# Linear-attention heads with tokens on the partitions behind the decay, in a two-block transformer kernel

## The chip, the cores and the metric

The kernel runs on one core of one Trainium2 chip. The metric is the device time of one execution in microseconds (us), as the median over runs. Engines are named as in the profile: PE (TensorE matmul), PEld (its weight loads), DVE (VectorE), ACT (ScalarE), SP (SyncE, which starts weight transfers).

## What is computed

The reference is a stack of two model blocks on one sequence of 256 tokens with 2048 features, all in float32. The first block's mixer projects the normed input by `w_in` into seven parts: `ka`, `qa`, `va`, `oa` for four linear-attention (mLSTM) heads of width 256 that run forward and backward in time, and `qb`, `kb`, `vb` for eight neighbourhood-attention heads. The change touches only the four mLSTM heads. In the closed form that the kernel uses, one head with the forward and the backward direction d is:

```
P_d[s, t] = (k_s . q_t) * scale * exp(col_d[s] + row_d[t])   for s <= t (d = forward), s >= t (d = backward), else 0
num_d[t, :] = sum_s P_d[s, t] * v[s, :]
den_d[t]    = sum_s P_d[s, t]
h[t, :] = sum_d num_d[t, :] / max(|den_d[t]|, exp(-m_d[t]))
out[t, :] = h[t, :] * rsqrt(mean(h[t, :]^2) + eps) * g_head * sigmoid(oa[t, :])
```

256 tokens are two chunks of 128. Of the four 128x128 blocks of P_d one is zero for each direction: keys in the later chunk against queries in the earlier for the forward direction, and the reverse for the backward.

## The kernel before

It is written engine by engine, with semaphores. Weights come as 412 **pieces** of 1 MB (128x2048). SP loads a piece into one of four `raw` slots when TensorE has finished the piece four before it. ACT's `split` rounds it to `w_hi` (L999), and DVE's `split` subtracts to get `w_lo` (L1412, on top of `raw`). TensorE multiplies each piece with the high and low halves of the activations. All three engines walk the same list of pieces. ACT and DVE call `begin(stage, j)` at each piece j; it does the split of the piece two ahead (`AHEAD = 2`) before anything else. ACT's split waits until TensorE has finished the piece before the present one (three `w_hi` slots). `begin` on DVE then also does the **ada** work placed at that piece by the table `ADA_AT`: the modulation vectors of later layers are matrix-vector products done on DVE, two instructions (L1425) for each 512 KB ada piece, one or two ada pieces at each weight piece, and at every eighth ada piece a transpose and a reduction more (L1431, L1432).

In a stage of columns (`ka`, `qa`, `qb`, `kb`, `oa`) each piece gives one bank of results. ACT copies half of it (`first_half`, L1018), and DVE adds the other half (`second_half`, L1465), which frees the bank. In a stage of tokens (`va`, `vb`) ACT evicts after four pieces, and DVE has no eviction.

Between the pieces stand the steps of the mLSTM heads. The table `A_STEPS` says behind which piece each step stands, on every engine: `scores`, `mix` and `norm` of head 0 at (va, 7), (qb, 1), (qb, 3), of head 1 at (qb, 4), (qb, 6), (kb, 0), of head 2 at (kb, 1), (kb, 3), (kb, 5), of head 3 at (kb, 6), (vb, 0), (vb, 2). The TensorE part of a step stands after the matmuls of that piece, the DVE part after its `second_half`, the ACT part after its `first_half`.

- `scores`: TensorE makes the products of k and q for both directions (L659), and spreads two rows of the gates over all partitions (L663: 512 columns, the row of the decay and the row of the bound). DVE adds the mask, ACT takes exponentials (L1072; L1074 for the bound), DVE multiplies by the scores (L1586). Keys are on the partitions.
- `mix`: TensorE multiplies `va` (stationary) with P (moving, 256 tokens) for the numerators (L680), and a block of ones with P for the denominators, which so stand on all 128 partitions (L676). Features are on the partitions. DVE then works on 128x512 tiles: bound, reciprocal, two products, sum, square (L1592 to L1598).
- `norm`: TensorE sums the squares over the partitions with a block of ones (L688). DVE makes the mean (L1602), ACT the root (L1078), DVE the reciprocal (L1604) and the product into `an` (L1606).

The neighbourhood-attention heads follow as waves from (vb, 3) on; the first (`b_wave(0)`, L721) waits until all four mLSTM heads are in `an`, because it reuses the PSUM banks `px`.

## Time and profile before

| | before |
|---|---|
| median of 3 runs | 2487.39 us (2486.23 to 2492.87) |
| the profiled execution | 2484.72 us |
| its span, first to last instruction | 2482.9 us |
| PE busy | 2375.4 us, 96% |
| DVE busy | 1996.0 us, 80% |
| ACT busy | 1109.2 us, 45% |
| granted TensorE clock, mean | 0.986 of full speed |

Times in rows are in us from the start of the span, unless marked ns. A timeline row has the start, the duration, the engine, the line, the operation, output<-inputs, shapes, and in brackets the idle time before it with what ended it; rows in sequence that are alike are merged (x4), and then the duration is that of all. A float32 matmul shows as two matmul records. A row of the stages has the stretch, its length, the busy time of each engine with the number of records, the granted clock (1.00 is 2.4 GHz, 0.50 is 1.2 GHz), the share of the DMA engines and GB/s. A row of groups has busy us and mean ns of one, and idle time before it. Ends of matmuls are modelled, so the distance between the starts of two rows tells how long the first took.

### The profile page before, as it was taken

The numbers are of one execution on the slowest core, as the hardware profiler recorded it, in microseconds if no ns is written. First come the engines' busy times: TensorE is split into PE (matmuls) and PEld (weight loads), VectorE is DVE, ScalarE is ACT, GpSimd is POOL, SyncE is SP. The second block draws the span as 40 slices with busy tenths as digits, with TensorE's granted clock in tenths as the row PEclk, the third lists the DMA queues.
The fourth block names the chain that finished last, engine by engine and source line by source line (L and its number), as shares of the span: only waits on it lengthen the run. The fifth ranks groups of instructions, "written<-read, shape, count | busy, mean of one in ns | idle before, by whom it ended". The sixth has DMA issues, their size and how long they took to land.

```text
span 2482.9 us, 31940 instructions
## 1 busy us (share of the span) xinstructions
PE 2375.4 (96%) x12936; PEld 2047.2 (82%) x12936; DVE 1996.0 (80%) x2481; ACT 1109.2 (45%) x1364; POOL 0.2 (0%) x4
## 2 busy tenths in 40 slices
PE   3599999998999999999998999999999998999999
PEld 3588887887888888888887788888888887888987
DVE  8999998899888888877787888787787666884764
ACT  1233434544445434454444444643545333555552
POOL 0000000000000000000000000000000000000000
PEclk9699999999999999999999999999999999999999
DMA  9889766685777688667685888776777775664343
GB/s 393 336 317 342 256 220 201 233 302 207 263 261 263 216 291 307 238 243 244 224 271 193 300 317 313 264 242 216 262 254 255 270 265 182 233 211 163 117 170 136
DMA packets 119010, 620.16 MB, mean 250 GB/s; under 512 B 13392, under 2 KB 14672, under 8 KB 76112
## 3 DMA queue, kind: packets, MB, share of 16 engines
q1 hardware_dynamic: 70560, 446.30, 51.3%
q10 hardware_dynamic: 48304, 171.82, 19.1%
q8 instruction: 102, 1.67, 0.3%
q14 instruction: 44, 0.36, 0.0%
HBM read 615.98 MB, written 2.10 MB: 249 GB/s over the span
## 4 chain that ended last, share of the span: by engine, by line
PE 72%; DVE 21%; DMA 3%; ACT 3%; issue 1%; ACTq 0%; SPq 0%; DVEq 0%
PE pm L536 20%; PE pm L537 10%; PE ps L536 10%; DVE w_lo L1412 7%; PE ps L537 5%; DVE acc L1425 5%; PE pm L575 4%; PE pm L576 4%; PE pm L577 4%; DMA ada<-in_ada 2%; ACT w_hi L999 2%; PE ps L575 2%; PE ps L577 2%; PE ps L576 2%; DVE acc_first L1478 1%
## 5 line engine op out<-in xcount | busy, mean ns | idle before, releaser
L1412 DVE TENSOR_TENSOR w_lo<-raw,w_hi 128x2048 fp32r<-128x2048 f32 (+2 forms) x412 | 892.0, 2165 | 296.1 <-ACT w_hi L999 294.4
L999 ACT ACTIVATE w_hi<-raw 128x2048 fp32r<-128x2048 f32 (+2 forms) x412 | 746.8, 1813 | 452.1 <-DMA raw<-in_w_down 128.3
L536 PE MATMUL pm<-h,w_hi 128*128 128x512 f32 x2350 | 832.6, 397 | 6.5 <-DVE w_lo L1412 6.3
L537 PE MATMUL pm<-h,w_lo 128*128 128x256 f32 x2350 | 658.0, 280 | 0.0
L536 PEld LDWEIGHTS pm<-h,w_hi 128*128 128x128 f32 x2350 | 440.9, 188 | 116.9 <-issue 13.0
L1425 DVE SCALAR_TENSOR_TENSOR acc<-ada,csil,acc 128x512 f32<-128x512 f32 x600 | 449.7, 749 | 12.6
L537 PEld LDWEIGHTS pm<-h,w_lo 128*128 128x128 f32 x2350 | 443.6, 189 | 0.2
L536 PE MATMUL ps<-h,w_hi 128*128 128x512 f32 x1202 | 426.4, 397 | 1.1 <-DVE w_lo L1412 1.0
L537 PE MATMUL ps<-h,w_lo 128*128 128x256 f32 x1202 | 336.5, 280 | 0.0
L536 PEld LDWEIGHTS ps<-h,w_hi 128*128 128x128 f32 x1202 | 225.5, 188 | 56.7 <-issue 3.6
L537 PEld LDWEIGHTS ps<-h,w_lo 128*128 128x128 f32 x1202 | 226.9, 189 | 0.1
L536 PE MATMUL pm<-glu,w_hi 128*128 128x512 f32 x484 | 170.5, 395 | 0.0
L575 PE MATMUL pm<-w_hi,h 128*128 128x512 f32 x352 | 138.9, 395 | 8.9 <-DVE h L1515 5.1
L576 PE MATMUL pm<-w_lo,h 128*128 128x512 f32 x352 | 137.8, 391 | 0.0
L577 PE MATMUL pm<-w_hi,h 128*128 128x512 f32 x352 | 137.6, 391 | 0.0
L537 PE MATMUL pm<-glu,w_lo 128*128 128x256 f32 x484 | 136.0, 281 | 0.0
L536 PEld LDWEIGHTS pm<-glu,w_hi 128*128 128x128 f32 x484 | 90.8, 188 | 21.7 <-DVE w_lo L1412 0.2
L537 PEld LDWEIGHTS pm<-glu,w_lo 128*128 128x128 f32 x484 | 91.1, 188 | 0.0
L591 PE MATMUL pv<-ones,acc_first 128*128 128x1 f32 x128 | 26.6, 338 | 66.5 <-DVE mods L1449 49.8
L1198 ACT ACTIVATE conv<-conv 128x256 f32<-128x256 f32 x44 | 18.4, 418 | 157.1 <-DVE conv L1715 157.1
L575 PEld LDWEIGHTS pm<-w_hi,h 128*128 128x128 f32 x352 | 66.6, 189 | 24.2 <-issue 5.5
L591 PEld LDWEIGHTS pv<-ones,acc_first 128*128 128x128 f32 x128 | 26.4, 313 | 66.8 <-DVE acc_first L1478 50.1
(403 smaller groups left out, 3100.8 us busy)
## 6 DMA issues: line engine op xcount, KB each, us to landing
ada<-in_ada ACTq DMA_DIRECT2D x320, 512.0 KB, 5.4
raw<-in_w_up SPq DMA_DIRECT2D x88, 1024.0 KB, 5.0
raw<-in_w_in SPq DMA_DIRECT2D x56, 1024.0 KB, 5.5
raw<-in_w_down SPq DMA_DIRECT2D x64, 704.0 KB, 5.0
raw<-in_sgu_v SPq DMA_DIRECT2D x32, 1024.0 KB, 6.0
raw<-in_sgu_u SPq DMA_DIRECT2D x32, 1024.0 KB, 5.2
raw<-in_sgu_z SPq DMA_DIRECT2D x32, 1024.0 KB, 4.9
raw<-in_sgu_out SPq DMA_DIRECT2D x32, 1024.0 KB, 4.9
```

Source lines behind the costliest of these rows:

```text
L536: pe.matmul(dst[:, :], wh[:, k, :], hl, start=(kc == 0), stop=False, skip_group_check=True)
L537: mm = pe.matmul(dst[:, 0:T], wl[:, k, :], hi, start=False, stop=last, skip_group_check=True)
L575: pe.matmul(dst[:, :], h_hi, wh[:, k, :], start=(kc == 0), stop=False, skip_group_check=True)
L576: pe.matmul(dst[:, :], h_hi, wl[:, k, :], start=False, stop=False, skip_group_check=True)
L577: mm = pe.matmul(dst[:, :], h_lo, wh[:, k, :], start=False, stop=(kc == 4 * parts - 1), skip_group_check=True)
L591: mm = pe.matmul(pv[:, c:c + 1], acc_first[:, u % 2, r, c * P:(c + 1) * P], ones[:, 0:1], start=(r == 0), stop=(r == 1))
L999: act.activation(w_hi[:, q % HSLOTS, 0:n], raw[:, q % SLOTS, 0:n], ACT.Copy).then_inc(hi_ready, 1)
L1198: act.activation(conv[:, k % 2, :], conv[:, k % 2, :], ACT.Gelu).then_inc(gelu_ready, 1)
L1412: tt_(w_lo[:, q % SLOTS, 0:n], raw[:, q % SLOTS, 0:n], whole(w_hi[:, q % HSLOTS, 0:n]), ALU.subtract).then_inc(lo_ready, 1)
L1425: ins = stt(dst, w, c, dst, ALU.mult, ALU.add)
L1478: ins = stt(dst, w, c, dst, ALU.mult, ALU.add)
```

## The change

Behind the decay the heads now have tokens on the partitions.

- `scores`: the bound no longer comes as a spread row. L663 has 256 columns instead of 512. The bound is turned once, by two more small transposes behind (ka, 7), and its exponential is taken once by ACT, at (qa, 0). L1074 is gone.
- `mix`: P is now the stationary operand, in 128x128 blocks, and `va` the moving one (256 columns). Each block is also multiplied with one column of ones, which gives the denominator as one column. The zero blocks are left out: 6 blocks a head instead of 8. DVE works on 128x4 for the denominators and with per-partition scalars on four 128x256 tiles.
- Squares and their sums are made by ACT (`accum_out`), in a new step `A_SQUARES` one piece after `mix`; ahead of ACT's `first_half` of that piece. Behind it DVE makes the mean (after its `second_half`), and ACT the root (after its `first_half`).
- `norm`: DVE makes a diagonal of the reciprocal roots (128x128 twice), ahead of its `second_half` of the norm's piece but behind its `begin`. TensorE multiplies h with the diagonal, which scales and turns it back to features on the partitions (four matmuls of 128 columns). DVE multiplies by `g_head`.

```diff
@@ -134,6 +134,7 @@
            ("kb", 6): ("scores", 3), ("vb", 0): ("mix", 3), ("vb", 2): ("norm", 3)}
+A_SQUARES = {("qb", 2): 0, ("qb", 7): 1, ("kb", 4): 2, ("vb", 1): 3}
 B_WAVES = {("vb", 3): 0, ("vb", 4): 1, ("vb", 5): 2, ("vb", 7): 3, ("oa", 0): 4, ("oa", 1): 5, ("oa", 2): 6, ("oa", 3): 7,
...
@@ -225,9 +226,10 @@
         bias_b = work("bias_b", [P, NH_B * 6, GRID_W], 14848)
-        expm = at_("expm", [P, 2, T], o_nt)
-        hf = at_("hf", [P, 2, T], o_nt + 2 * T)
-        bcol = at_("bcol", [P, TT, GROW], o_ssq)
+        diag_a = at_("diag_a", [P, TT, P], o_nt)
+        hf = at_("hf", [P, TT, DH_A], o_nt + 2 * T)
+        bcol = at_("bcol", [P, 2, TT, GROW], o_ssq + 160)
+        small_a = at_("small_a", [P, 4, 4], o_ssq + 304)
         wmask = at_("wmask", [P, GRID_W], o_ssq + 80)
...
@@ -653,14 +658,14 @@
                 else:
-                    pe.wait_ge(a_sq, hd_)
+                    pe.wait_ge(a_hf, hd_)
                 for sc in range(TT):
                     for dc in range(2):
                         pe.matmul(px[0][:, sc * T:(sc + 1) * T], ka[:, 2 * hd_ + dc, sc * P:(sc + 1) * P],
                                   qa[:, 2 * hd_ + dc, :], start=(dc == 0), stop=(dc == 1))
                 for d in range(2):
                     r = hd_ + 32 * d
-                    mm = pe.matmul(px[1 + d][:, :], ident[0:GROW, r:r + 1].to_broadcast([GROW, P]), neg_rows[0:GROW, :],
+                    mm = pe.matmul(px[1 + d][:, 0:T], ident[0:GROW, r:r + 1].to_broadcast([GROW, P]), neg_rows[0:GROW, 0:T],
                                    start=True, stop=True)
...
@@ -670,23 +675,25 @@
                 else:
-                    pe.wait_ge(a_ms, hd_)
-                for d in range(2):
-                    for sc in range(TT):
-                        pe.matmul(px[3][:, d * T:(d + 1) * T], ones[:, :], decay[:, d, sc * T:(sc + 1) * T],
-                                  start=(sc == 0), stop=(sc == 1))
-                    for ec in range(2):
-                        for sc in range(TT):
-                            mm = pe.matmul(px[1 + d][:, ec * T:(ec + 1) * T],
-                                           va[:, sc, hd_ * DH_A + ec * P:hd_ * DH_A + (ec + 1) * P],
-                                           decay[:, d, sc * T:(sc + 1) * T], start=(sc == 0), stop=(sc == 1))
+                    pe.wait_ge(a_out, hd_)
+                for tc in range(TT):
+                    for d in range(2):
+                        seen = range(tc + 1) if d == 0 else range(tc, TT)
+                        for sc in seen:
+                            first, last = sc == seen[0], sc == seen[-1]
+                            probs = decay[:, d, sc * T + tc * P:sc * T + (tc + 1) * P]
+                            pe.matmul(px[3][:, 2 * tc + d:2 * tc + d + 1], probs, ones[:, 0:1], start=first, stop=last)
+                            mm = pe.matmul(px[1 + d][:, tc * DH_A:(tc + 1) * DH_A], probs, va[:, sc, hd_ * DH_A:(hd_ + 1) * DH_A],
+                                           start=first, stop=last)
                 mm.then_inc(a_num, 1)
 
             def a_head_norm(hd_):
-                pe.wait_ge(a_sq, hd_ + 1)
+                pe.wait_ge(a_diag, hd_ + 1)
                 for ec in range(2):
-                    mm = pe.matmul(px[3][:, 0:T], ones[:, :], hb[:, ec, :], start=(ec == 0), stop=(ec == 1))
-                mm.then_inc(a_ss, 1)
+                    for tc in range(TT):
+                        mm = pe.matmul(px[3][:, ec * T + tc * P:ec * T + (tc + 1) * P], hf[:, tc, ec * P:(ec + 1) * P], diag_a[:, tc, :],
+                                       start=True, stop=True)
+                mm.then_inc(a_turned, 1)
 
...
@@ -729,7 +736,9 @@
                     for sc in range(TT):
-                        mm = pe.transpose(px[1][:, sc * GROW:(sc + 1) * GROW], gates[0:GROW, 5, sc * P:(sc + 1) * P],
+                        pe.transpose(px[1][:, sc * GROW:(sc + 1) * GROW], gates[0:GROW, 5, sc * P:(sc + 1) * P],
+                                     ident[0:GROW, 0:GROW])
+                        mm = pe.transpose(px[1][:, (TT + sc) * GROW:(TT + sc + 1) * GROW], neg_rows[0:GROW, T + sc * P:T + (sc + 1) * P],
                                           ident[0:GROW, 0:GROW])
...
@@ -1069,13 +1078,19 @@
                     for sc in range(TT):
-                        act.activation(decay[:, d, sc * T:(sc + 1) * T], decay[:, d, sc * T:(sc + 1) * T], ACT.Exp,
-                                       bias=bcol[:, sc, r:r + 1])
-                    act.activation(expm[:, d, :], px[1 + d][:, T:2 * T], ACT.Exp).then_inc(a_exp, 1)
-
-            def a_head_norm(hd_):
+                        ex = act.activation(decay[:, d, sc * T:(sc + 1) * T], decay[:, d, sc * T:(sc + 1) * T], ACT.Exp,
+                                            bias=bcol[:, 0, sc, r:r + 1])
+                    ex.then_inc(a_exp, 1)
+
+            def a_head_squares(hd_):
+                act.wait_ge(a_hf, hd_ + 1)
+                for tc in range(TT):
+                    sq = act.activation(hb[:, tc, :], hf[:, tc, :], ACT.Square, accum_out=small_a[:, 1, tc:tc + 1])
+                sq.then_inc(a_sq, 1)
+
+            def a_head_root(hd_):
                 act.wait_ge(a_ms, hd_ + 1)
-                act.activation(expm[:, 0, :], expm[:, 0, :], ACT.Sqrt).then_inc(a_std, 1)
+                act.activation(small_a[:, 2, 0:TT], small_a[:, 2, 0:TT], ACT.Sqrt).then_inc(a_std, 1)
 
...
@@ -1113,9 +1128,10 @@
                     b_exponent(B_WAVES[part, j] - 1)
+                if (part, j) in A_SQUARES:
+                    a_head_squares(A_SQUARES[part, j])
                 if (part, j) == ("vb", 0):
                     act.wait_ge(rows_ready, 1)
-                    act.wait_ge(bcol_ready, 1)
                 if (part, j) == ("oa", 6):
...
@@ -1136,9 +1152,13 @@
                     mix_high(hx[:, 2:4, 0:T], ob, 2)
-                if (part, j) in A_STEPS and A_STEPS[part, j][0] != "mix":
-                    step, k = A_STEPS[part, j]
-                    {"scores": a_head_scores, "norm": a_head_norm}[step](k)
+                if (part, j) == ("qa", 0):
+                    act.wait_ge(bcol_ready, 1)
+                    act.activation(flat(bcol[:, 1, :, :]), flat(bcol[:, 1, :, :]), ACT.Exp).then_inc(ecol_ready, 1)
+                if (part, j) in A_STEPS and A_STEPS[part, j][0] == "scores":
+                    a_head_scores(A_STEPS[part, j][1])
+                if (part, j) in A_SQUARES:
+                    a_head_root(A_SQUARES[part, j])
                 if (part, j) in B_WAVES:
...
@@ -1571,7 +1591,7 @@
                     dve.wait_ge(bcol_ps, 1)
-                    dve.tensor_copy(flat(bcol[:, :, :]), px[1][:, 0:2 * GROW]).then_inc(bcol_ready, 1)
+                    dve.tensor_copy(bcol[:, :, :, :].rearrange("p a b c -> p (a b c)"), px[1][:, 0:4 * GROW]).then_inc(bcol_ready, 1)
 
...
@@ -1587,23 +1607,36 @@
                 dve.wait_ge(a_num, hd_ + 1)
-
-                em = flat(expm[:, :, :])
-                chain.link(stt(em, px[3][:, :], -1.0, em, ALU.mult, ALU.max))
-                chain.link(tt_(em, px[3][:, :], em, ALU.max))
-                chain.link(dve.reciprocal(em, em))
-                tt_(hf[:, :, :], halves(px[1][:, :]), over(expm[:, 0, :], 2), ALU.mult)
-                chain.link(tt_(hb[:, :, :], halves(px[2][:, :]), over(expm[:, 1, :], 2), ALU.mult))
-                chain.link(tt_(hf[:, :, :], hf[:, :, :], hb[:, :, :], ALU.add))
-                tt_(hb[:, :, :], hf[:, :, :], hf[:, :, :], ALU.mult).then_inc(a_sq, 1)
+                if hd_ == 0:
+                    dve.wait_ge(ecol_ready, 1)
+                den, bound = halves(px[3][:, 0:4]), bcol[:, 1, :, hd_:hd_ + 33:32]
+                norm = halves(small_a[:, 0, :])
+                chain.link(stt(norm, den, -1.0, bound, ALU.mult, ALU.max))
+                chain.link(tt_(norm, den, norm, ALU.max))
+                chain.link(dve.reciprocal(small_a[:, 0, :], small_a[:, 0, :]))
+                for tc in range(TT):
+                    ins = ts_(hf[:, tc, :], px[1][:, tc * DH_A:(tc + 1) * DH_A], small_a[:, 0, 2 * tc:2 * tc + 1], None, ALU.mult)
+                chain.link(ins)
+                for tc in range(TT):
+                    ins = stt(hf[:, tc, :], px[2][:, tc * DH_A:(tc + 1) * DH_A], small_a[:, 0, 2 * tc + 1:2 * tc + 2], hf[:, tc, :],
+                              ALU.mult, ALU.add)
+                ins.then_inc(a_hf, 1)
+
+            def a_head_mean(hd_):
+                dve.wait_ge(a_sq, hd_ + 1)
+                ts_(small_a[:, 2, 0:TT], small_a[:, 1, 0:TT], 1.0 / DH_A, EPS, ALU.mult, ALU.add).then_inc(a_ms, 1)
+
+            def a_head_diagonal(hd_):
+                dve.wait_ge(a_std, hd_ + 1)
+                chain.link(dve.reciprocal(small_a[:, 3, 0:TT], small_a[:, 2, 0:TT]))
+                for tc in range(TT):
+                    ins = ts_(diag_a[:, tc, :], ident[:, :], small_a[:, 3, tc:tc + 1], None, ALU.mult)
+                ins.then_inc(a_diag, 1)
 
             def a_head_norm(hd_):
-                dve.wait_ge(a_ss, hd_ + 1)
-                ts_(expm[:, 0, :], px[3][:, 0:T], 1.0 / DH_A, EPS, ALU.mult, ALU.add).then_inc(a_ms, 1)
-                dve.wait_ge(a_std, hd_ + 1)
-                chain.link(dve.reciprocal(expm[:, 0, :], expm[:, 0, :]))
+                dve.wait_ge(a_turned, hd_ + 1)
                 for ec in range(2):
-                    ins = stt(an[:, 2 * hd_ + ec, :], hf[:, ec, :], pcol("ghead", 2 * hd_ + ec), expm[:, 0, :], ALU.mult, ALU.mult)
+                    ins = ts_(an[:, 2 * hd_ + ec, :], px[3][:, ec * T:(ec + 1) * T], pcol("ghead", 2 * hd_ + ec), None, ALU.mult)
                 ins.then_inc(a_out, 1)
...
@@ -1653,6 +1686,8 @@
                     chain.link(tt_(bias_b[:, :, :], bias_b[:, :, :], over(wmask[:, :], NH_B * 6), ALU.add))
+                if (part, j) in A_STEPS and A_STEPS[part, j][0] == "norm":
+                    a_head_diagonal(A_STEPS[part, j][1])
                 if (part, j) == ("oa", 7):
...
@@ -1665,6 +1700,8 @@
                     {"scores": a_head_scores, "mix": a_head_mix, "norm": a_head_norm}[step](k)
+                if (part, j) in A_SQUARES:
+                    a_head_mean(A_SQUARES[part, j])
                 if (part, j) in B_WAVES and B_WAVES[part, j] < NH_B:
```

Two places show where the steps now stand. The first is ACT's queue at head 0, from the split at (qb, 2) to the split at (qb, 3); `w_hi<-raw` is a split, `qb<-pm` a `first_half`, `ada<-in_ada` the start of an ada transfer. Before:

```order
L999 ACTIVATE w_hi<-raw 128x2048 [waits slot_full0,piece_done]
L1004 DMA ada<-in_ada 128x1024 [waits ada_used]
L1018 ACTIVATE qb<-pm 128x256 [waits piece_done]
L999 ACTIVATE w_hi<-raw 128x2048 [waits slot_full1,piece_done]
L1004 DMA ada<-in_ada 128x1024 [waits ada_used]
L1018 ACTIVATE qb<-ps 128x256 [waits piece_done]
L1078 ACT_TABLE_LOAD
L1078 ACTIVATE expm<-expm 128x256 [waits a_ms]
```

and with the change:

```order
L1008 ACTIVATE w_hi<-raw 128x2048 [waits slot_full0,piece_done]
L1013 DMA ada<-in_ada 128x1024 [waits ada_used]
L1088 ACTIVATE sqt,small_a<-hf 128x256 [waits a_hf]
L1088 ACTIVATE sqt,small_a<-hf 128x256
L1027 ACTIVATE qb<-pm 128x256 [waits piece_done]
L1093 ACT_TABLE_LOAD
L1093 ACTIVATE small_a<-small_a 128x2 [waits a_ms]
L1008 ACTIVATE w_hi<-raw 128x2048 [waits slot_full1,piece_done]
```

The root, which waits for DVE's mean (`a_ms`), now stands ahead of the second split, where it stood behind it; the two squares (they write `sqt` as a by-product) stand ahead of the `first_half`.

The second is DVE's queue, from the split at (qb, 3) to the next split; `w_lo<-raw` is a split, `acc<-ada` the ada work, `qb<-qb` a `second_half`, `qa` is where `an` lies. Before:

```order
L1412 TENSOR_TENSOR w_lo<-raw,w_hi 128x2048 [waits hi_ready]
L1425 SCALAR_TENSOR_TENSOR acc<-ada,csil,acc 128x512 [waits ada_full2]
L1425 SCALAR_TENSOR_TENSOR acc<-ada,csil,acc 128x512 [waits dve_step]
L1465 TENSOR_TENSOR qb<-qb,ps 128x256 [waits half_out,ada_used]
L1602 TENSOR_SCALAR expm<-px 128x256 [waits a_ss]
L1604 RECIPROCAL expm<-expm 128x256 [waits a_std]
L1606 SCALAR_TENSOR_TENSOR qa<-hf,par,expm 128x256 [waits dve_step]
L1606 SCALAR_TENSOR_TENSOR qa<-hf,par,expm 128x256
L1412 TENSOR_TENSOR w_lo<-raw,w_hi 128x2048 [waits hi_ready]
```

and with the change, from the mean at (qb, 2) on:

```order
L1627 TENSOR_SCALAR small_a<-small_a 128x2 [waits a_sq]
L1432 TENSOR_TENSOR w_lo<-raw,w_hi 128x2048 [waits hi_ready]
L1445 SCALAR_TENSOR_TENSOR acc<-ada,csil,acc 128x512 [waits ada_full2]
L1445 SCALAR_TENSOR_TENSOR acc<-ada,csil,acc 128x512 [waits dve_step]
L1631 RECIPROCAL small_a<-small_a 128x2 [waits a_std,ada_used]
L1633 TENSOR_SCALAR diag_a<-ident,small_a 128x128 [waits dve_step]
L1633 TENSOR_SCALAR diag_a<-ident,small_a 128x128
L1485 TENSOR_TENSOR qb<-qb,ps 128x256 [waits half_out]
L1639 TENSOR_SCALAR qa<-px,par 128x256 [waits a_turned]
L1639 TENSOR_SCALAR qa<-px,par 128x256
```

The diagonal stands behind a split and the ada work, and the two products into `qa` behind a wait for TensorE's turn. TensorE's own place of the norm's matmuls, behind the piece (qb, 3), is as before; they waited for the squares made in `mix` and now wait for the diagonal.

## Rows read from the trace of the kernel before

**Rows 1.** Busy time in the mLSTM stretch: PE, PEld, DVE, ACT, POOL, clock, DMA

```profile
250.00:410.00 160.00, 156.00 (x788) 129.32 (x787) 146.62 (x157) 66.63 (x77) 0.00 (x0) 0.99 0.67 235
```

**Rows 2.** Timeline of PE: start of the piece (qb, 3), and what follows it

```profile
277.09 0.39 PE L536 MATMUL ps<-h,w_hi 128*128 128x512 f32 x1
...
282.64 1.03 PE L688 MATMUL px<-sqt,ones 128*128 128x256 f32 x4
```

**Rows 3.** What PE waited for, 380 to 410: total us, times, longest

```profile
PE px L721 <- ACT vb L1132: 2.4, 1, 2.4
PE pm L575 <- DVE w_lo L1412: 1.1, 1, 1.1
PE px L688 <- DVE sqt L1598: 0.5, 1, 0.5
```

**Rows 4.** Timeline of PE: end of scores of head 0, mix of head 1

```profile
253.04 1.98 PE L663 MATMUL px<-neg_rows,ident 36*128 36x512 f32 x4
254.95 0.50 PE L536 MATMUL ps<-h,w_hi 128*128 128x512 f32 x1
...
304.30 1.02 PE L676 MATMUL px<-decay,ones 128*128 128x256 f32 x4
...
309.29 0.58 PE L536 MATMUL pm<-h,w_hi 128*128 128x512 f32 x1
```

**Rows 5.** Timeline of PE near 57: float32 matmuls of one column, full clock

```profile
56.66 1.84 PE L591 MATMUL pv<-ones,acc_first 128*128 128x1 f32 x16
```

**Rows 6.** Timeline of DVE at head 1, (qb, 6) to (kb, 0)

```profile
309.67 0.69 DVE L1592 SCALAR_TENSOR_TENSOR expm<-px,expm 128x512 f32<-128x512 f32 x1
...
317.17 2.29 DVE L1412 TENSOR_TENSOR w_lo<-raw,w_hi 128x2048 fp32r<-128x2048 f32 x1
319.37 1.54 DVE L1425 SCALAR_TENSOR_TENSOR acc<-ada,csil,acc 128x512 f32<-128x512 f32 x2
...
322.41 0.42 DVE L1465 TENSOR_TENSOR qb<-qb,pm 128x256 f32<-128x256 f32 x1
322.75 2.28 DVE L1412 TENSOR_TENSOR w_lo<-raw,w_hi 128x2048 fp32r<-128x2048 f32 x1
324.95 0.48 DVE L1423 TENSOR_SCALAR acc<-ada,csil 128x512 f32<-128x512 f32 x1
...
327.83 0.42 DVE L1465 TENSOR_TENSOR kb<-kb,pm 128x256 f32<-128x256 f32 x1
```

**Rows 7.** Timeline of ACT at head 0, (qb, 2) to (qb, 4)

```profile
277.29 0.38 ACT L1018 ACTIVATE qb<-pm 128x256 f32<-128x256 f32 x1 [7.15 <-PE pm L537]
...
288.23 1.90 ACT L999 ACTIVATE w_hi<-raw 128x2048 fp32r<-128x2048 f32 x1
```

**Rows 8.** Groups of DVE by form: eviction with a scalar, diagonal

```profile
L1602 DVE TENSOR_SCALAR expm<-px 128x256 f32<-128x256 f32 x4 | 1.7, 419 | 0.0
...
L1832 DVE TENSOR_SCALAR diag<-ident,stat 128x128 f32<-128x128 f32 x4 | 1.1, 286 | 0.1
```

**Rows 9.** Timeline of ACT, then of DVE, at wave 0: table load, tiny reciprocal

```profile
411.80 1.28 ACT L1101 ACT_TABLE_LOAD   x1 [2.18 <-DVE acc L1425]
413.15 0.51 ACT L1101 ACTIVATE s_b<-s_b,small_b 128x256 f32<-128x256 f32 x1
...
415.22 0.16 DVE L1615 RECIPROCAL small_b<-small_b 128x2 f32<-128x2 f32 x1
```

**Rows 10.** Short stretches around three waits of PE; the granted clock is third from the end

```profile
406.00:407.00 1.00, 0.00 (x0) 0.00 (x0) 0.96 (x2) 1.00 (x2) 0.00 (x0) 0.99 0.49 164
...
412.00:414.00 2.00, 2.00 (x7) 1.57 (x6) 1.93 (x4) 1.93 (x4) 0.00 (x0) 0.55 0.76 207
...
1352.00:1354.00 2.00, 0.00 (x0) 0.00 (x0) 1.96 (x2) 0.00 (x0) 0.00 (x0) 0.62 0.00 0
...
1358.00:1360.00 2.00, 2.00 (x8) 1.58 (x7) 2.00 (x6) 1.80 (x2) 0.00 (x0) 0.68 0.00 0
...
1379.00:1381.00 2.00, 0.34 (x2) 0.00 (x0) 2.00 (x1) 1.72 (x1) 0.00 (x0) 1.00 0.98 385
```

5 lines of the change are left out of this document (4 added, 1 removed).

## The prediction

> **What bounds the kernel now.** I read the page's first part (the table above): TensorE is the busiest engine by far. Then the stage, since the average says nothing of it: from 250 to 410 us, where nearly all the mLSTM work lies, TensorE is busy for 156 of 160 us, DVE for 146.6, ACT for 66.6 [rows 1]. So TensorE is the bound there and DVE is close behind it; DVE's work counts only where TensorE waits for it. The waits of TensorE in this stage add up to 4.0 us and all lie near the end [rows 3]: 0.5 us for the squares of head 3, 1.1 us for a `w_lo` that DVE made late, 2.4 us before wave 0. The last is put down to ACT's eviction, but that wave also waits for head 3 in `an`, DVE's last product of the norm, which the code names (`a_out`). All three come from DVE being late.
>
> That last wait costs more than its length. The granted clock is still 0.99 in 406 to 407, and 0.55 in 412 to 414, which is full speed again from about 413.7 on [rows 10]. So it was granted 1.2 instead of 2.4 GHz from 407.0 to 413.7. TensorE had stopped near 405.5 and worked again from 407.9: 5.8 us of work at half speed, 2.9 us lost. Another wait, at 1352 to 1358, shows the same length: 0.62 in one stretch and 0.68 in the other put the low clock from 1352.5 to 1359.3, some 6.8 us [rows 10]. A third, shorter one, with TensorE idle for 1.7 of the 2 us from 1379, keeps 1.00 [rows 10].
>
> **The change, part by part. TensorE's own work.**
> - Scores: L663 takes 1.90 us a head, from 253.04 to the next row [rows 4]; half the columns, half the time: -0.95 a head, -3.8.
> - Mix: from 304.30 to 309.29 it takes 4.99 us for 24 records of 256 columns, 0.208 each [rows 4]. Now 6 blocks have 12 such records, 2.5 us, and 12 records of one column. A train of 16 of those took 1.84 us, 0.115 each [rows 5]: 1.4 us. Sum 3.9, so -1.1 a head, -4.4. Were the short ones hidden behind the long ones, it would be 2.5 (-2.5 a head), and that is the lower bound; the upper is 0.208 for all 24 records, no gain. I take 0.115, the row of the same shape.
> - The Trainium skill, page "TensorE: Matmul & The Clock Gate", section "Back-to-back issue gap", gives small matmuls an issue floor of some 25 ns. By it the mix would be about 2.8 us (an estimate from the page); the row, at 115 ns, speaks against it, since each record here also loads 128 columns of float32 weights.
> - Norm: 4 records of 256 columns become 8 of 128, 0.9 us either way. The two extra transposes at (ka, 7) cost about 0.2 us. Together: -3.8 - 4.4 + 0.2 = -8.0 us.
>
> **DVE's work.** The mix on DVE lasts from 309.67 to 317.17, 7.5 us [rows 6]. Now: three operations on 128x4 at about 0.2 (the tiny reciprocal takes 0.16 [rows 9]), and four passes of 128x256 at 0.42 [rows 8] with the ends overlapping: 2.25 us. The norm loses a 1.75 us reciprocal too. DVE gets some 7 us a head lighter, and is then never late at the three waits above: -4.0 and -2.9 of clock, -6.9 us.
>
> **The new wait.** This is the part that decides. Until now TensorE needed for the norm only the squares that DVE made within `mix`, two pieces earlier. Now it needs the diagonal, and between the mix and the diagonal stand two of DVE's `begin`s, two trips to ACT and one of ACT's splits: the order shows DVE's mean, then ACT's root, and behind the root ACT's split, for which DVE's next split waits, then the ada work, then the diagonal. For head 1, from the end of TensorE's mix:
> - DVE: mix 2.25; split 2.2; ada work of (qb, 7) with transpose and reduction 3.0 (319.37 to 322.41); `second_half` 0.35; mean 0.2 [rows 6, 9]: 8.0.
> - ACT: root of 128x2 about 0.2, its table load being done meanwhile; split 1.9 [rows 7]: 10.1.
> - DVE: split 2.2; ada work of (kb, 0) 2.9 (324.95 to 327.83) [rows 6]; tiny reciprocal 0.2 [rows 9]; two diagonals 0.29 each, overlapping, 0.5 [rows 8]: 15.9.
> - TensorE meanwhile: two pieces of 5.55 (277.09 to 282.64) [rows 2] and some 0.1, 11.2.
>
> So TensorE waits for 4.7 us at head 1. Head 2 has two whole ada pieces (3.1) in the first `begin` and 3.0 in the second: 5.0. Head 0 has one ada piece each time (1.5), but DVE comes 1.2 us late to its mix from work before: 3.2. At head 3 the pieces are of the `vb` kind, and DVE and ACT don't wait for a `first_half` there: 2.25 + 2.2 + 1.5 + 0.2 + 0.2, ACT's split 1.9, DVE's 2.2, ada 1.5, diagonal 0.7 is 12.7, against two pieces of 5.44: 1.8. Sum +14.7 us. Nothing hides these: the norm's matmuls stand in TensorE's queue ahead of the next piece. ACT's squares (0.5 each [rows 9]) end before its `first_half` is due, and the extra exponential at (qa, 0), 0.3 us, falls in a stage where ACT is idle for more than half: no cost; were that cover gone, it would be 0.3 us and a table load, 1.6.
>
> A page differs here: the Trainium skill, "ScalarE: Activation LUTs", section "What ACT_TABLE_LOAD costs", gives 2.66 us for a change of table, load and drain. By that the root would be late by itself and the waits about 3 us longer in all (an estimate from the page). The row shows 1.28 us, and the next activation starts 0.07 us after its end [rows 9], so I go by that.
>
> **The clock.** If each wait longer than 2.4 us is followed by the low clock, and it lasts 6.7 us from some 1.6 us into the wait (1.5 after 405.5), then a wait of s leaves 6.7 - (s - 1.6) of work at half speed: half of that is 2.55 for head 0, 1.8 for head 1, 1.65 for head 2, nothing for head 3 (1.8 us is like the wait that kept 1.00). Sum +6.0. Bounds: 0 if it never falls, and 4 x 2.9 = 11.6 if each costs what the one before wave 0 cost.
>
> **Sum.** -8.0 - 6.9 + 14.7 + 6.0 = +5.8 us. Behind the stage the engines stand as before, TensorE going from piece to piece, so it is carried to the end. Against the profiled execution, 2484.72 us, that is 2490.5; the median of the runs shown lies 2.7 us above that execution, so 2493.2 us for the median. A measurement of this kernel can tell about 0.3%, 7.5 us, from no change. I forecast no measurable change, a little on the slow side.
>
> **Rivals.**
> - A, slower: the clock. The wait is as forecast, but at each of the four norms the clock falls and stays low through the norm and half of the next piece. For it: the one comparable wait in a stage dense with pieces, of 2.4 us, cost 2.9. Against: longer waits use up part of the low time. It gives +5.8 - 6.0 + 11.6 = +11.4 us, 2498.8. It decides from a low time of about 4 us of work after each wait.
> - B, faster: the wait is not there. If the diagonal came by the time that TensorE ends the norm's piece, only the savings are left: -8.0 - 6.9 = -14.9 us, 2472.5. For it: DVE sheds 7 us a head and could be well ahead. Against: being ahead doesn't help, as the root can't come before the piece before is evicted and DVE's split waits for ACT's. From the end of that piece it is at least 0.2 (ACT starts at 277.29 what TensorE ended at 277.09 [rows 2, 7]), 0.4 + 0.4 + 0.2 + 0.2 (both halves, mean, root), 1.9, 2.2, 1.5 and 0.7, together 7.7, against 5.55 of the norm's piece.
> - C, the one-column records are hidden behind the long ones, the lower bound above: the mix takes 2.5 us, -1.4 a head more, of which head 0 gives its part back in waiting: +5.8 - 4.2 = +1.6 us, 2489.0. Against it: the train of sixteen [rows 5]. The rule of the Trainium skill's page on TensorE would come near this.
>
> **How the numbers follow.** The forecast, 2487 to 2496: 0.52. A: 0.30. B: 0.10. C: 0.08. Of the forecast's 0.52 some 0.08 lies over the 7.5 us bound. So faster 0.10 (B), within 0.3% 0.44 + 0.08 = 0.52, slower 0.30 + 0.08 = 0.38. For the range I take in the forecast, C and A: the lower end is the waits with no clock lost, 5.8 - 6.0 = -0.2, and half of C's gain, 2485, rounded down to 2484 for a first wait that is shorter; the upper is A and 2 us more for DVE's small operations, 2501. B is left out.
>
> **What would show it.** Right: a wait of TensorE at the norm's matmuls (L694 in the changed code) for DVE's diagonal, four times, 2 to 5 us; the three waits of [rows 3] gone; the granted clock at 0.5 after the longer ones; DVE's busy time in the stage down by some 27 us; the mix at 3.9 us. Wrong: no such wait, or one under 1 us, would make it B. A wait that moves to `w_lo` behind the norm would say that ACT's split, held up by the root, is late for TensorE too.

## Result and the profile after

| | before | changed |
|---|---|---|
| median | 2487.68 us (2486.23 to 2492.87, 6 runs) | 2496.45 us (2492.77 to 2499.75, 6 runs) |
| ratio to before, 95% interval | | 1.0031 [1.0021, 1.0041] |
| the profiled execution | 2484.72 us | 2492.77 us |
| its span | 2482.9 us | 2490.9 us |
| DVE busy | 1996.0 us | 1969.7 us |
| granted clock, mean | 0.986 | 0.984 |

The changed kernel is slower by 8.8 us, 0.31 to 0.35%: in the range, 3.3 us above the forecast, just past the 0.3% that I called no measurable change, and 0.45 us over the upper end of the forecast's own 2487 to 2496. By its number it stands a little nearer to rival A (2498.8) than to the forecast (2493.2). What PE waited for in the changed kernel from 240 to 430 us is one line (total us, times, longest), in the place of the three of [rows 3]:

```profile
PE px L694 <- DVE diag_a L1633: 15.6, 4, 5.0
```

The stretches of the changed kernel, with the columns of [rows 1] and [rows 10]; the first answers to [rows 1]:

```profile
250.00:410.00 160.00, 144.44 (x763) 123.19 (x762) 117.98 (x161) 65.04 (x82) 0.00 (x0) 0.96 0.64 220
284.00:286.00 2.00, 1.40 (x10) 1.30 (x10) 1.04 (x5) 0.00 (x0) 0.00 (x0) 0.91 0.98 311
286.00:288.00 2.00, 2.00 (x8) 1.71 (x7) 2.00 (x3) 0.00 (x0) 0.00 (x0) 0.50 0.40 160
288.00:290.00 2.00, 2.00 (x11) 1.78 (x10) 1.97 (x3) 0.00 (x0) 0.00 (x0) 0.74 0.00 0
327.00:329.00 2.00, 1.92 (x9) 1.92 (x10) 0.36 (x2) 0.00 (x0) 0.00 (x0) 0.50 0.85 207
329.00:331.00 2.00, 2.00 (x10) 1.72 (x10) 1.80 (x3) 0.00 (x0) 0.00 (x0) 0.75 0.50 195
...
369.00:371.00 2.00, 1.49 (x7) 1.49 (x8) 0.79 (x3) 0.00 (x0) 0.00 (x0) 0.50 0.54 123
371.00:373.00 2.00, 2.00 (x8) 1.80 (x8) 1.37 (x3) 0.00 (x0) 0.00 (x0) 0.50 0.35 139
373.00:375.00 2.00, 2.00 (x9) 1.66 (x8) 2.00 (x2) 0.00 (x0) 0.00 (x0) 0.66 0.00 0
```

DVE is busy for 28.6 us less in 250 to 410. Not all of that is relief, since less of the stage's work now falls into that stretch: over the whole kernel DVE is busy for 26.3 us less (1996.0 to 1969.7), 6.6 us a head, where about 7 were foreseen. TensorE stands still for 15.6 of the 160 us, where it stood for 4. The third number from the end is the clock. Behind the waits at heads 0, 1 and 2 (work resumes at 284.60, 327.08 and 369.51) it is at 0.50, which is 1.2 GHz, up to about 289.0, 330.0 and 374.4. The work done in that time lost half of it: 1.7, 1.45 and 2.4 us, in all 5.6. Behind head 3's wait of 2.0 us it did not fall.

The timeline of PE in the changed kernel, at the mix of head 0 and then at the norm of head 1:

```profile
265.51 0.28 PE L685 MATMUL px<-ones,decay 128*128 128x1 f32 x2
265.65 0.68 PE L686 MATMUL px<-va,decay 128*128 128x256 f32 x2
266.17 0.28 PE L685 MATMUL px<-ones,decay 128*128 128x1 f32 x2
...
269.25 0.58 PE L541 MATMUL pm<-h,w_hi 128*128 128x512 f32 x1
```

```profile
327.08 2.08 PE L694 MATMUL px<-diag_a,hf 128*128 128x128 f32 x8 [4.88 <-DVE diag_a L1633]
328.81 0.77 PE L541 MATMUL ps<-h,w_hi 128*128 128x512 f32 x1
```

The mix now takes 3.74 us (4.99 in [rows 4]): from start to start, 0.14 us for the pair of one-column records of a block and 0.52 for the pair of 256 columns. The turn at the norm took 1.73 us here, at the low clock; at head 0, with the clock at 1.00, it took 0.92, and the norm's matmuls before took 0.68 (282.64 to 283.32).

Now the chain that makes TensorE wait, at head 1. DVE in the changed kernel:

```profile
311.14 0.16 DVE L1614 SCALAR_TENSOR_TENSOR small_a<-px,bcol 128x4 f32<-128x4 f32 x1 [2.85 <-PE px L686]
...
313.45 2.28 DVE L1432 TENSOR_TENSOR w_lo<-raw,w_hi 128x2048 fp32r<-128x2048 f32 x1
...
319.02 0.16 DVE L1627 TENSOR_SCALAR small_a<-small_a 128x2 f32<-128x2 f32 x1
321.26 2.29 DVE L1432 TENSOR_TENSOR w_lo<-raw,w_hi 128x2048 fp32r<-128x2048 f32 x1 [2.08 <-ACT w_hi L1008]
323.47 0.48 DVE L1443 TENSOR_SCALAR acc<-ada,csil 128x512 f32<-128x512 f32 x1
323.99 2.33 DVE L1445 SCALAR_TENSOR_TENSOR acc<-ada,csil,acc 128x512 f32<-128x512 f32 x3
326.35 0.17 DVE L1631 RECIPROCAL small_a<-small_a 128x2 f32<-128x2 f32 x1
326.55 0.48 DVE L1633 TENSOR_SCALAR diag_a<-ident,small_a 128x128 f32<-128x128 f32 x2
```

and ACT beside it:

```profile
316.69 0.39 ACT L1027 ACTIVATE qb<-pm 128x256 f32<-128x256 f32 x1 [2.21 <-PE pm L542]
317.10 1.28 ACT L1093 ACT_TABLE_LOAD   x1
319.22 0.20 ACT L1093 ACTIVATE small_a<-small_a 128x2 f32<-128x2 f32 x1 [0.84 <-DVE small_a L1627]
...
319.33 1.90 ACT L1008 ACTIVATE w_hi<-raw 128x2048 fp32r<-128x2048 f32 x1
```

The root is done at 319.4. The diagonal, which needs only the root, starts at 326.35: DVE idles for 2.08 us for ACT's split, does its own split (2.2 us) and four ada instructions (2.9), because the diagonal stands behind them in its queue. TensorE had ended its piece at 322.2. DVE was idle 2.85 us before the mix, so it is not overloaded at this head.

**Where the time went.** I take the stage from the first product of q and k to the start of wave 0, in the timeline of PE: 251.2 to 407.9 before, 251.2 to 416.8 now, 156.7 against 165.6 us, +8.9. Its terms, measured: scores 4 x (1.05 - 1.91) = -3.4; mix 4 x (3.74 - 4.99) = -5.0; the old waits gone, -4.0; the new ones +15.6; low clock +5.6. Sum +8.8. Not in it is the turn, 0.1 to 0.2 us a head longer than the norm's matmuls before, which is within what the pieces themselves differ by. Behind the stage the low clock after the wait before wave 0 (2.9 us) is gone. The spans differ by +8.0, so 2.0 us are left over, which lie at places that the change does not touch.

### The profile page after: what moved, and what is told of

It reads as the page before. It is cut to its first block, busy times and chain, and to the rows that moved or that the text cites. A ratio compares the mean times of both kernels' runs of the same rounds, so it can differ in the third digit from the quotient of the medians.

```text
span 2490.9 us, 31993 instructions
## 1 busy us (share of the span) xinstructions
PE 2372.5 (95%) x12954; PEld 2047.8 (82%) x12954; DVE 1969.7 (79%) x2489; ACT 1112.8 (45%) x1373; POOL 0.2 (0%) x4
## 4 chain that ended last, share of the span: by engine, by line
PE 75%; DVE 18%; DMA 3%; ACT 2%; issue 1%; ACTq 0%; SPq 0%; DVEq 0%
PE pm L541 21%; PE pm L542 11%; PE ps L541 11%; DVE w_lo L1432 7%; PE ps L542 5%; PE pm L580 4%; PE pm L581 4%; PE pm L582 4%; DVE acc L1445 4%; ACT w_hi L1008 2%; DMA ada<-in_ada 2%; PE ps L580 2%; PE ps L581 2%; PE ps L582 2%; DVE nt L1527 1%
## 5 line engine op out<-in xcount | busy, mean ns | idle before, releaser
L1445 DVE SCALAR_TENSOR_TENSOR acc<-ada,csil,acc 128x512 f32<-128x512 f32 x600 | 449.4, 749 | 12.6
L1218 ACT ACTIVATE conv<-conv 128x256 f32<-128x256 f32 x44 | 18.5, 420 | 157.2 <-DVE conv L1752 157.2
```

The source lines that it names most:

```text
L1218: act.activation(conv[:, k % 2, :], conv[:, k % 2, :], ACT.Gelu).then_inc(gelu_ready, 1)
L1445: ins = stt(dst, w, c, dst, ALU.mult, ALU.add)
```

## Experiments

Times taken at different hours are compared by their ratios to the kernel before, which ran beside each. The stage is measured as above, in one profiled execution of each version; two versions without a wait in it (e1 and e10) agree within 0.02 us. A "load" is unused work that only costs its engine time; where edits start from e1, that is said.

| run | median, us | ratio to before | stage, us | waits for the diagonal, us |
|---|---|---|---|---|
| changed kernel | 2496.45 | 1.0031 [1.0021, 1.0041] | 165.6 | 15.6 |
| e1_diag_early | 2471.46 | 0.9932 [0.9911, 0.9952] | 144.0 | 0 |
| e2_norm_two_pieces_later | 2491.72 | 1.0009 [0.9998, 1.0021] | 162.9 | 11.8 |
| e3_filler_in_wait | 2491.46 | 1.0008 [0.9999, 1.0018] | 159.9 | 3.2 |
| e4_diag_before_ada | 2480.73 | 0.9960 [0.9946, 0.9974] | 152.0 | 5.5 |
| e2b_norm_later_diag_stays | 2475.55 | 0.9952 [0.9934, 0.9969] | 146.4 | 2.0 |
| e5_zero_blocks_back | 2479.85 | 0.9969 [0.9956, 0.9982] | 148.6 | 0 |
| e6_spread_bound_back | 2475.63 | 0.9953 [0.9939, 0.9968] | 147.4 | 0 |
| e7_dve_load_back | 2500.71 | 1.0055 [1.0035, 1.0074] | 171.1 | 18.5 |
| e8_dve_load_behind_norm | 2493.04 | 1.0020 [1.0011, 1.0030] | 156.2 | 6.4 |
| e9_load_behind_norm_not_head3 | 2486.02 | 0.9988 [0.9979, 0.9998] | 156.0 | 6.0 |
| e10_half_load_behind_norm | 2473.44 | 0.9938 [0.9922, 0.9954] | 144.0 | 0 |

### Is it the wait, and is the wait a matter of order? (e1)

The diagonal behind the mean, one piece earlier in DVE's queue; nothing else:

```diff
-                if (part, j) in A_STEPS and A_STEPS[part, j][0] == "norm":
-                    a_head_diagonal(A_STEPS[part, j][1])
...
                     a_head_mean(A_SQUARES[part, j])
+                    a_head_diagonal(A_SQUARES[part, j])
```

> The changed kernel, with DVE making the diagonal right behind the mean, one piece earlier, ahead of the next split and ada work. Theory (the diagonal is late because it stands behind a split and the ada work): TensorE's four waits at the norm (3.7, 4.9, 5.0, 2.0 us, 15.6 in all) are gone, with them the low clock behind three of them (about 4.7 us): some 20 us faster than the changed kernel, about 2476 us, and 11 to 12 us faster than before. Rival 1 (the time is in the one-column matmuls and the turn, not in the wait): no difference, 2496. Rival 2 (DVE now waits about 1 us for ACT's root at each head, and its splits come late): waits for w_lo of 1 us or more appear in the stage and only half is regained, about 2486.

The timeline of DVE in e1 at head 1, and the stretch that answers to [rows 1]:

```profile
314.79 0.16 DVE L1627 TENSOR_SCALAR small_a<-small_a 128x2 f32<-128x2 f32 x1
315.22 0.17 DVE L1631 RECIPROCAL small_a<-small_a 128x2 f32<-128x2 f32 x1 [0.27 <-ACT small_a L1093]
315.42 0.48 DVE L1633 TENSOR_SCALAR diag_a<-ident,small_a 128x128 f32<-128x128 f32 x2
```

```profile
250.00:410.00 160.00, 159.91 (x865) 136.54 (x863) 135.11 (x189) 73.72 (x96) 0.00 (x0) 1.00 0.70 249
```

DVE waits 0.27 us for the root and makes the diagonal at once, 2.1 us before TensorE gets there (318.02). No wait of TensorE is left, the clock is 1.00, and the stage is 21.5 us shorter than in the changed kernel, which is the waits (15.6) and the low clock (5.6) and 0.3 more. The version is faster than both: 0.9932 of before. Its median, 2471.46, is 4.5 us below what I expected; 0.9 of that is clock that I had counted too low, and the rest lies for the most part behind the stage, at places that the edit does not touch.

### The rest of the chain (e2, e2b, e4)

e2 gives the norms of heads 0 to 2 two pieces more. The diagonal moves along, since it is tied to the norm's piece:

```diff
-A_STEPS = {("va", 7): ("scores", 0), ("qb", 1): ("mix", 0), ("qb", 3): ("norm", 0),
-           ("qb", 4): ("scores", 1), ("qb", 6): ("mix", 1), ("kb", 0): ("norm", 1),
-           ("kb", 1): ("scores", 2), ("kb", 3): ("mix", 2), ("kb", 5): ("norm", 2),
+A_STEPS = {("va", 7): ("scores", 0), ("qb", 1): ("mix", 0), ("qb", 5): ("norm", 0),
+           ("qb", 4): ("scores", 1), ("qb", 6): ("mix", 1), ("kb", 2): ("norm", 1),
+           ("kb", 1): ("scores", 2), ("kb", 3): ("mix", 2), ("kb", 7): ("norm", 2),
```

> The changed kernel with the norm of heads 0, 1 and 2 placed two pieces later, order within DVE's queue as in the changed kernel. Theory: two pieces are 11 us, more than the longest wait of 5.0, so the waits of heads 0 to 2 (13.6 us) and the low clock behind them (4.7) are gone, that of head 3 (2.0) stays: about 18 us faster than the changed kernel, 2478. Rival (something in the turned norm itself is slow, or DVE's split behind ACT's root makes w_lo late for TensorE): no gain, 2494 or more.

A miss. The waits shrink by 3.8 us only; what PE waited for in e2 from 240 to 430:

```profile
PE px L694 <- DVE diag_a L1633: 11.8, 4, 3.6
```

The root had been ready for two pieces (278.9 at head 0, and the diagonal began at 298.58), so the chain from mix to root does not set these waits. What sets them is local: the diagonal stands behind the split and the ada work of the norm's own piece, and that split waits for ACT's. In e2 each norm now follows the piece of the next head's `scores`, so ACT's split in its turn stands behind the four exponentials of the decay. At head 0, ACT and then DVE in e2:

```profile
292.47 0.49 ACT L1081 ACTIVATE decay<-decay,bcol 128x256 f32<-128x256 f32 x1
292.87 1.90 ACT L1008 ACTIVATE w_hi<-raw 128x2048 fp32r<-128x2048 f32 x1
```

```profile
294.81 2.29 DVE L1432 TENSOR_TENSOR w_lo<-raw,w_hi 128x2048 fp32r<-128x2048 f32 x1 [1.12 <-ACT w_hi L1008]
297.01 1.53 DVE L1445 SCALAR_TENSOR_TENSOR acc<-ada,csil,acc 128x512 f32<-128x512 f32 x2
298.58 0.17 DVE L1631 RECIPROCAL small_a<-small_a 128x2 f32<-128x2 f32 x1
```

Time given to the chain's head is worth nothing behind that. To check this, e2b makes the same move and leaves the diagonal at its old pieces:

```diff
+A_DIAGONALS = {("qb", 3): 0, ("kb", 0): 1, ("kb", 5): 2, ("vb", 2): 3}
...
-                if (part, j) in A_STEPS and A_STEPS[part, j][0] == "norm":
-                    a_head_diagonal(A_STEPS[part, j][1])
+                if (part, j) in A_DIAGONALS:
+                    a_head_diagonal(A_DIAGONALS[part, j])
```

> As e2_norm_two_pieces_later, in which the diagonal had moved along with the norm and still stood behind that piece's split and ada work. Here the diagonal stays at its piece of the changed kernel, and only TensorE's turn and what follows it stand two pieces later. Theory (the time that counts is from the diagonal's begin to the turn, not from the mix): the waits of heads 0 to 2 are gone, that of head 3 (2.0 us) stays: 2478 or less. Rival (the norm must follow within the same pieces for another reason): 2491 as e2.

```profile
PE px L695 <- DVE diag_a L1634: 2.0, 1, 2.0
```

That is the only wait of PE in the stage in e2b, at head 3, which was not moved. Its median, 2475.55, is within what I expected. So what counts is how far the diagonal stands ahead of the turn, not how far the turn stands behind the mix. e4 leaves the diagonal at the norm's piece, but behind the split and ahead of the ada work:

```diff
+                urgent = (lambda: b_scale(w - 1)) if 0 < w <= NH_B else None
+                if (part, j) in A_STEPS and A_STEPS[part, j][0] == "norm":
+                    urgent = lambda: a_head_diagonal(A_STEPS[part, j][1])
-                begin(part, j, (lambda: b_scale(w - 1)) if 0 < w <= NH_B else None)
+                begin(part, j, urgent)
```

> The changed kernel, with the diagonal behind the norm's split but ahead of its ada work. Theory: each wait is shorter by the ada work of its piece, 1.5, 2.9, 3.0 and 1.5 us, so 2.2, 2.0, 2.0 and 0.5 are left, 8.9 us less, and some 2 to 4 of the 4.7 us of clock too: about 2485. If the wait came from ACT's split alone, with the ada work hidden beside it, nothing is gained: 2496.

Measured 0.9960, with this as PE's wait from 240 to 430:

```profile
PE px L694 <- DVE diag_a L1633: 5.5, 4, 1.9
```

So putting the diagonal ahead of the ada work took away 10.1 of the 15.6 us (8.9 expected), and 5.5 remain with the root and the splits. The median is 4 us below what I expected, about half of that in the stage. The clock is 0.99 in 250 to 410 where it was 0.96, and the stage is 13.5 us shorter: 10.1 of wait, and 3.4 that I put down to the clock. The trace bears that out head by head: from the turn to the next q and k product, heads 0 and 2 take 6.55 us each, as in e1 (6.44), where the changed kernel took 8.11 and 8.82. At head 1 they take 8.21, for there the clock was low again, from 322.3 to 325.7, behind a wait of only 1.8 us.

### What the low clock costs (e3)

TensorE runs unused float32 matmuls of 256 columns in the wait (16 records for heads 0 to 2, 8 for head 3):

```diff
+                pe.wait_ge(a_hf, hd_ + 1)
+                for _ in range(8 if hd_ < 3 else 4):
+                    pe.matmul(px[3][:, 0:T], ones[:, :], va[:, 0, 0:T], start=True, stop=True)
                 pe.wait_ge(a_diag, hd_ + 1)
```

> The changed kernel, with matmuls that nothing uses put in front of the norm's wait: 8 of 256 float32 columns at heads 0 to 2 (3.4 us), 4 at head 3 (1.7 us). They fill idle time and add no work beyond it. If the low clock behind the waits comes from TensorE idling there, it stays at full speed and about 4.7 us come back: 2491.7. If the low clock is not from the idling, no gain: 2496, or 1 us more where the filler outlasts the wait.

The timeline of PE in e3 at head 1, and two stretches of e3 there:

```profile
321.46 3.61 PE L693 MATMUL px<-va,ones 128*128 128x256 f32 x16
326.29 1.16 PE L697 MATMUL px<-diag_a,hf 128*128 128x128 f32 x8 [1.22 <-DVE diag_a L1636]
```

```profile
327.00:329.00 2.00, 2.00 (x15) 1.77 (x14) 1.51 (x3) 0.00 (x0) 0.00 (x0) 1.00 0.81 262
329.00:331.00 2.00, 2.00 (x13) 1.76 (x12) 2.00 (x2) 0.00 (x0) 0.00 (x0) 1.00 0.08 33
```

The norm can start no earlier than before (at head 0 the unused matmuls even outlast the diagonal, by 0.4 us), and the clock is 1.00 where it was 0.50. The stage gets 5.7 us shorter and the median falls by 5.0: the share of the clock in the loss, by itself, against the 5.6 read from the stretches.

### What the saved TensorE work is worth (e5, e6)

Both start from e1, where TensorE is never idle in the stage. e5 computes the two zero blocks again, e6 spreads 512 columns instead of 256:

```diff
-                        seen = range(tc + 1) if d == 0 else range(tc, TT)
+                        seen = range(TT)
```

> e1_diag_early with the zero blocks computed again: 8 blocks a head instead of 6, each 0.14 us for the column and 0.52 for the 256 columns in the trace of the changed kernel. Nothing waits in that stage, so TensorE's time counts in full: 4 heads x 2 x 0.66 = 5.2 us slower than e1_diag_early, 2476.7. If the matmuls were hidden behind DVE there, 0.

```diff
-                    mm = pe.matmul(px[1 + d][:, 0:T], ident[0:GROW, r:r + 1].to_broadcast([GROW, P]), neg_rows[0:GROW, 0:T],
+                    mm = pe.matmul(px[1 + d][:, :], ident[0:GROW, r:r + 1].to_broadcast([GROW, P]), neg_rows[0:GROW, :],
```

> e1_diag_early with L663's 512 columns again instead of 256, so that the row of the bound is spread and not used. Theory: 0.95 - 0.1 = 0.85 us a head (1.91 against 1.05 in the traces), 3.4 us slower than e1_diag_early, 2474.9. If hidden: 0.

In the stage e5 costs 4.6 us and e6 3.4, both near what was expected, and no wait comes up in either. In e5 each mix takes 1.32 us longer (5.06 against 3.74), 5.3 in all, as expected; at heads 0 to 2 the two pieces behind it took 0.2 us less than in e1 (11.28 against 11.50), and why stays open. The median of e6 (+4.2 us on e1) agrees. That of e5 (+8.4) is 3.8 us above its stage; the two ratios differ by 0.0037 with some 0.0024 either way, so 4.6 us lies within. The last section says why the stage is the better measure here.

### DVE's weight and its place (e7 to e10)

Was the lighter DVE worth the 6.9 us of old waits? e7 puts four unused reciprocals of 128x256, 7.0 us, behind the mix of each head in e1:

```diff
                 ins.then_inc(a_hf, 1)
+                for _ in range(4):
+                    chain.link(dve.reciprocal(waste[:, :], ones[:, 0:1].to_broadcast([P, T])))
```

> e1_diag_early with four reciprocals of 128x256 (1.75 us each, 7.0 a head) that nothing uses, put on DVE behind the mix's last product: about the DVE work that the change took away. The stage took 144 us in e1_diag_early with DVE busy for some 122 of it; 28 more make 150. Theory (DVE's relief was worth the three waits of before and their clock, 6.9 us): TensorE waits again for what DVE makes late, 5 to 9 us slower than e1_diag_early, 2476 to 2480. If DVE's load does not count: 2471.5.

A miss by over 20 us, and my own oversight: the load stands between the mix and the mean, inside the chain. What PE waited for in e7, 240 to 430:

```profile
PE px L695 <- DVE diag_a L1636: 18.5, 4, 5.1
```

The stage is 27.0 us longer than in e1: 18.5 of waits, and for most of the rest low clock behind those of heads 0 to 2. The chain of e1 at head 1 runs from 306.5, the end of TensorE's mix, to 315.9: 9.4 us of the 11.5 that two pieces take. It has 2.1 us of slack, and 7.0 - 2.1 = 4.9 is about each of the waits (4.7, 5.1, 5.0, 3.6). e8 has the same load behind the norm's last product, outside the chain:

```diff
                 ins.then_inc(a_out, 1)
+                for _ in range(4):
+                    chain.link(dve.reciprocal(waste[:, :], ones[:, 0:1].to_broadcast([P, T])))
```

> The same 7.0 us of unused DVE work a head as in e7 (four reciprocals of 128x256), now right behind the norm's last product instead of right behind the mix, so outside the chain mix, squares, mean, root, diagonal. Question: does DVE's weight a head cost time (the -6.9 us that I gave to a lighter DVE), or only its place in the chain (e7: 18.5 us of waits for the diagonal)? Theory 'place and weight are two things': DVE has 135.1 us of work in the 160 us of the stage in e1, with 28 more it is full (163), so it falls behind there and a few waits come back, now for w_lo (L1432) or for the mean's consumers, 4 to 8 us in all with or without some us of low clock: about 2476 to 2481 us, waits at the norm below 3 us in all. Rival 'weight alone decides': the same waits as e7, near 2500 us. Rival 'slack hides it all': DVE is ahead by the two pieces of its splits and nothing waits, 2471 to 2473 us; then the -6.9 us was never due to DVE's weight but to where the mix stood.

It took 2493 us, 12 us over the upper end of what I had given to the weight, and the waits at the norm came to 6.4 us, not below 3. One part was a matter of head 3, whose load stood right ahead of the softmax of wave 0 (a wait of 5.8 us for `s_b`, at most 0.6 in e7, e9 and e10). e9 leaves it out there, e10 also halves the rest (both against e8):

```diff
-                for _ in range(4):
+                for _ in range(4 if hd_ < 3 else 0):
```

```diff
-                for _ in range(4):
+                for _ in range(2 if hd_ < 3 else 0):
```

> e8 without the load at head 3: in e8 that load (7.1 us of DVE work right ahead of wave 0's softmax) led to a wait of 5.8 us for s_b and to low clock behind it, which is a matter of the neighbourhood heads and not of DVE's weight in the stage. Left: 7.0 us a head for heads 0 to 2. In e8 the stage from the first q.k matmul to the first wave took 156.3 us against 144.1 in e1, so +12 for the weight. Theory (a full DVE falls behind at its splits and at the mix, and TensorE waits for it): about +9 us against e1, 2480 us, and no wait for s_b of that size. Rival (all of e8's loss came from head 3's place): within 2 us of e1, 2473 us.

> As e9 with two reciprocals a head in place of four (3.5 us of unused DVE work behind the norm of heads 0 to 2). If the loss comes from DVE being full, half the load costs much less than half: DVE then has 125.4 + 10.5 = 135.9 us of work in 150, and the backlog of 3.5 us is gone before the next mix: 0 to 2 us above e1, 2471.5 to 2473.5 us. If each us of DVE work costs time, it is half of what e9 loses, some 2476 us.

What PE waited for in e9 from 240 to 440, and in e10 in the same stretch:

```profile
PE px L695 <- DVE diag_a L1634: 6.0, 3, 2.3
PE pm L542 <- DVE w_lo L1433: 1.5, 1, 1.5
```

```profile
PE px L707 <- DVE s_b L1653: 0.6, 1, 0.6
```

The stretch 250 to 400, first of e9 and then of e10:

```profile
250.00:400.00 150.00, 142.80 (x768) 121.31 (x766) 136.00 (x171) 61.53 (x81) 0.00 (x0) 0.99 0.68 234
```

```profile
250.00:400.00 150.00, 150.00 (x820) 128.64 (x819) 134.90 (x177) 70.57 (x89) 0.00 (x0) 1.00 0.72 250
```

3.5 us a head cost the stage nothing (144.0 against 144.0), and e10's median is what I expected. 7.0 us a head cost it 11.9, and e9's median is 6 us above what I expected: 7.5 of waits, and for much of the rest low clock (at 0.50 in two stretches, below). Both have DVE at 90% of the stretch, but e9 does less in it: with 21 us on e1's 121 in a stage of 144 there is some 98% of the time spoken for, DVE must still wait for ACT's splits (8.9 us in the stage), and it falls behind. At head 1 it came to the mix at 311.83, 4.1 us later than in e1 when both are counted from the q and k product, and so the load ends up in the same chain as in e7. So the first 10.5 us of load were free and the next 10.5 cost 11.9; where between 3.5 and 7.0 us a head the cost begins was not measured.

That the kernel before was past this point is argued and not shown. Its DVE was busy for 91% of its stage (143.3 of 156.7 us, e10 90% without a wait), which alone tells little. Where its waits lie, at head 3, the trace says more: DVE came to the mix at 389.12, 4.1 us after TensorE had ended it, and worked with only 0.48 us of pause until wave 0 began. Two of its rows there have no counterpart in the changed kernel, where the reciprocals are of 128x4 and 128x2:

```profile
390.58 3.35 DVE L1594 RECIPROCAL expm<-expm 128x512 f32<-128x512 f32 x1
405.08 1.75 DVE L1604 RECIPROCAL expm<-expm 128x256 f32<-128x256 f32 x1 [0.48 <-ACT expm L1078]
```

No run puts a load back at these two places of head 3 alone.

## Why the prediction came out as it did

It held in its mechanism and in most sizes; that the clock's sum and the mix came out so near is in part luck, as said below. By its steps, measured against forecast:

- **Scores**: -3.4 for -3.8. A head saves 0.86 rather than 0.95: the spread now takes 1.05 us from start to start, not half of 1.90.
- **Mix**: -5.0 for -4.4. A one-column pair takes 0.14 us between pairs of 256 columns, where I took 0.23 from the train of sixteen; and a pair of 256 columns took 0.52, where I had 0.42. The two errors nearly cancel (3.74 us for 3.9). Rival C, in which the short records are free, had 2.5 us and fell by this. The floor of the Trainium skill ("TensorE: Matmul & The Clock Gate", "Back-to-back issue gap"), some 25 ns, or some 62 with hardware decode off, is not reached here either: 70 ns a record. Which of the two figures would apply to this kernel no run here shows.
- **The old waits**: gone, as said, -4.0 and the 2.9 of clock behind them. That this was DVE's weight is supported, and not shown, by e9 and e10: a DVE that is 7 us heavier at heads 0 to 2 makes TensorE wait for it, one that is 3.5 heavier doesn't. But those waits are for the diagonal and for a `w_lo` at heads 0 to 2, not the old three at head 3.
- **Norm and transposes**: taken as even, the turn is 0.12 us a head longer than the norm's matmuls before at full clock (0.80 in e1 against 0.68). The 0.2 us for the two transposes does not show: the stage starts at 251.22 and 251.23.
- **The new wait**: 3.7, 4.9, 5.0 and 2.0 us for 3.2, 4.7, 5.0 and 1.8; 15.6 for 14.7. The step by step addition was right in what ends last, and e4, e2 and e2b take it apart. What I had not carried on is that under this chain lies a second one, local to the norm's piece (the argument that I used against rival B). I had expected e2 to remove the wait, and it took away only 3.8 us. How much shorter the second chain is in the changed kernel itself stays open, for in e2 it also holds the exponentials of the next head.
- **The table load**: 1.28 us, and the root then waited 0.84 us more for DVE's mean, so the load was no part of the chain. By the Trainium skill ("ScalarE: Activation LUTs", "What ACT_TABLE_LOAD costs"), 2.66 us with the drain, the root would have started at 319.76; it started at 319.22, and the trace disagrees with the page here.
- **The clock**: 5.6 for 6.0 by the stretches, 5.0 to 5.7 by e3. The split over the heads was off: 1.7, 1.45, 2.4 for 2.55, 1.8, 1.65. I had let the clock fall 1.6 us into each wait longer than 2.4 us and stay low for 6.7 us; it was low for 3.4 us at heads 0 and 1 and for 6.8 at head 2. So that rule does not hold from wait to wait, and that its sum came out right is luck. A loss as large as A's, four times 2.9, was not there; of the 4 us of work at low clock behind each wait that A asks for, there were 3.4, 2.9, 4.9 and 0. So A's number is near, and its mechanism is not what happened.
- **Not in the sum**: +2.0 us of the spans at places that the change doesn't touch. Without them the spans differ by 6.0, near the 5.8 of the forecast; with them by 8.0, and the rest of the 8.8 is the difference between the profiled executions and the medians. That puts the result on the edge of "no measurable change".
- **Rival B** was the right alternative. Its time, 2472.5, is that of e1 (2471.46). What it lacked was the order: with the diagonal in its present place it can't happen, and one piece earlier it does.

## What to carry to other kernels

When a matmul comes to wait for a small result that crosses two engines, look at what stands in the queue ahead of its last instruction rather than at the lengths: here 0.7 us of DVE work stood behind 7 us of idle time and work that it did not need, and moving it one piece up turned +8.8 us into -17.1 (medians of the changed kernel and of e1 against the kernel before; in the stage +8.9 into -12.6). A saving on an engine that is not the bound is worth time only up to where it stops being late; a load put back in two sizes tells between which two that point lies. And a step to which you give more room gains only if the instruction that it waits for doesn't move with it.
